# First MLP product of an encoder block: each weight tile's products written as three 256-column matmuls into half a bank, and the addition of two halves left out

## The reference

```
x  = x + merged @ w_out
h2 = rms_norm(x, g_mlp)
x  = x + jnp.square(jax.nn.relu(h2 @ w_mlp_in)) @ w_mlp_out
out = rms_norm(x, g_final)
```

## Time and profile before

| | |
|---|---|
| median of 3 runs | 1630.17 us (1629.72 to 1630.33) |
| the profiled execution | 1630.46 us |
| its span, first to last instruction | 1628.6 us |
| PE busy | 1616.6 us (99%), 7974 matmuls |
| PEld busy | 1361.0 us (84%) |
| DVE busy | 1215.4 us (75%) |
| ACT busy | 898.4 us (55%) |
| granted TensorE clock, mean | 0.999 of full speed |

### The profile page before, as it was taken

How to read it: one execution, slowest core, us unless ns; L and a number is a source line. 1 busy time by engine, 2 the same in 40 slices (tenths; PEclk the granted TensorE clock), 3 DMA queues, 4 the chain that set the end, 5 groups by cost and what they waited for, 6 DMA issues and landing times.

```text
span 1628.6 us, 20399 instructions
## 1 busy us (share of the span) xinstructions
PE 1616.6 (99%) x7974; PEld 1361.0 (84%) x7974; DVE 1215.4 (75%) x1470; ACT 898.4 (55%) x1248; POOL 79.0 (5%) x67
## 2 busy tenths in 40 slices
PE   9999999999999999999999999999999999999998
PEld 7888888888888888888888888888888888888886
DVE  7887778877666677766565567996699768986793
ACT  6666656766565445554444555654565455555562
POOL 3000000000000134000000000000000000000000
PEclk9999999999999999999999999999999999999999
DMA  7666665666556664445565775457635863576461
GB/s 270 193 207 201 187 188 188 206 195 205 174 186 185 190 186 154 143 143 179 182 234 193 259 235 190 157 206 235 190 125 202 273 190 130 207 262 189 144 233 52
DMA packets 134192, 312.19 MB, mean 192 GB/s; under 512 B 9744, under 2 KB 10448, under 8 KB 133968
## 3 DMA queue, kind: packets, MB, share of 16 engines
q1 hardware_dynamic: 129376, 302.21, 56.8%
q10 hardware_dynamic: 4720, 8.68, 2.1%
HBM read 308.68 MB, written 2.16 MB: 191 GB/s over the span
## 4 chain that ended last, share of the span: by engine, by line
PE 87%; DVE 9%; issue 2%; DMA 1%; ACT 1%; POOL 0%; POOLq 0%; ACTq 0%; DVEq 0%
PE G L1599 18%; PE G L1600 17%; PE G L1601 17%; PE S L1608 7%; PE G L1608 7%; PE G L1612 4%; PE S L1612 4%; PE S L1599 3%; PE S L1601 3%; PE S L1600 3%; DVE wlo L951 3%; DVE wlo_late L951 2%; PE S L1620 1%; DMA raw<-in_w_in 1%; DVE raw L954 1%
## 5 line engine op out<-in xcount | busy, mean ns | idle before, releaser
L602 ACT ACTIVATE whi<-raw 128x1024 fp32r<-128x1024 f32 x377 | 398.4, 1060 | 395.7 <-PE G L1601 317.0
L951 DVE TENSOR_TENSOR wlo<-raw,whi 128x1024 fp32r<-128x1024 f32 x377 | 461.0, 1236 | 133.6 <-ACT whi L602 132.8
L1599 PE MATMUL G<-whi,a_both 128*128 128x512 f32 x960 | 376.8, 393 | 2.2 <-DVE wlo L951 2.2
L1601 PE MATMUL G<-whi,a_both 128*128 128x512 f32 x960 | 373.8, 389 | 0.0
L1600 PE MATMUL G<-wlo,a_both 128*128 128x512 f32 x960 | 373.8, 389 | 0.0
L1599 PEld LDWEIGHTS G<-whi,a_both 128*128 128x128 f32 x960 | 180.3, 188 | 39.9 <-issue 2.8
L1601 PEld LDWEIGHTS G<-whi,a_both 128*128 128x128 f32 x960 | 180.2, 188 | 37.8
L1600 PEld LDWEIGHTS G<-wlo,a_both 128*128 128x128 f32 x960 | 180.4, 188 | 35.7
L1599 PE MATMUL G<-whi,b_hi 128*128 128x512 f32 x328 | 128.5, 392 | 0.3
L1600 PE MATMUL G<-wlo,b_hi 128*128 128x512 f32 x328 | 128.0, 390 | 0.0
L1601 PE MATMUL G<-whi,b_lo 128*128 128x512 f32 x328 | 127.7, 389 | 0.0
(11 more groups left out here) (283 smaller groups left out, 2591.7 us busy)
## 6 DMA issues: line engine op xcount, KB each, us to landing
raw<-in_w_in SPq DMA_DIRECT2D x208, 512.0 KB, 4.1
raw<-in_w_mlp_in SPq DMA_DIRECT2D x64, 512.0 KB, 4.3
gates<-in_w_mlp_in SPq DMA_DIRECT2D x64, 512.0 KB, 3.7
raw<-in_w_mlp_out SPq DMA_DIRECT2D x64, 512.0 KB, 4.9
gates<-in_w_mlp_out SPq DMA_DIRECT2D x64, 512.0 KB, 4.9
raw<-in_w_ssm_up SPq DMA_DIRECT2D x32, 512.0 KB, 3.6
raw<-in_w_attn_up SPq DMA_DIRECT2D x32, 512.0 KB, 4.0
raw<-in_w_out SPq DMA_DIRECT2D x32, 512.0 KB, 4.6
```

Of the source, the lines that this page charges most:

```text
L602: act.activation(high(m), piece(n), ACT.Copy).then_inc(hi_made, 1)
L951: dve.tensor_tensor(low(m), piece(n), high(m).bitcast(F32), ALU.subtract).then_inc(lo_made, 1)
L1599: pe.matmul(out_ap, hi[:, k, cols], w_hi, start=start, stop=False)
L1601: return pe.matmul(out_ap, lo[:, k, cols], w_hi, start=False, stop=stop)
```

## The change

`weights_first` now issues, for each tile c and contraction step kk, three matmuls of 256 moving columns into the first half of the bank: high weights by `a_hi`, high weights by `a_lo`, low weights by `a_hi`. The second half of each bank is no longer used. ACT's copy of it (L887), DVE's addition of the halves (L1382) and their semaphores `hid_t` and `h_taken` are gone. DVE's maximum and product (L1384) reads PSUM itself and waits for the window's matmuls itself, and PE's waits for free banks are on `hid_v`. The scratch tile `s_sum` shares `tmp_a` with the copy that is gone; the wait that guarded it moved from ACT to DVE, ahead of the sums of the blocks.

```diff
         def hidden(p, idx, pr, pp):
             g, j = idx
-            if p == 0:
-                act.wait_ge(used, done(pr, pp))
-                if g or j > CROSSED[0]:
-                    act.wait_ge(s_lo_made, len(CROSSED) * g + sum(u < j for u in CROSSED))
-                act.activation(hidden_t, hidden_banks(j)[:, :, T:2 * T], ACT.Copy).then_inc(hid_t, 1)
             if p == 1:
...
         def hidden(p, idx, pr, pp):
             g, j = idx
             if p == 0:
-                dve.wait_ge(hid_t, g * 4 + (j + 1))
+                dve.wait_ge(used, done(pr, pp))
                 if 4 * g + j:
                     dve.wait_ge(hid_lo, g * 4 + j)
                 dve.wait_ge(hid_hi, g * 4 + (j + 1))
-                dve.tensor_tensor(hidden_u, hidden_t, hidden_banks(j)[:, :, 0:T], ALU.add).then_inc(h_taken, 1)
-                dve.wait_ge(h_taken, g * 4 + (j + 1))
-                dve.scalar_tensor_tensor(out=hidden_u, in0=hidden_u, scalar=0.0,
+                dve.scalar_tensor_tensor(out=hidden_u, in0=hidden_banks(j)[:, :, 0:T], scalar=0.0,
                                          in1=rstd_row[:, :].unsqueeze(1).to_broadcast([P, 4, T]),
                                          op0=ALU.max, op1=ALU.mult).then_inc(hid_v, 1)
...
-                turn = 4 * (len(CROSSED) * g + CROSSED.index(j))
+                before = len(CROSSED) * g + CROSSED.index(j)
+                turn = 4 * before
+                if before:
+                    dve.wait_ge(s_lo_made, before)
...
             for c in range(4):
-                cols = [slice(kk * N + c * P, kk * N + (c + 1) * P) for kk in range(2)]
                 for kk in range(2):
-                    pe.matmul(banks[:, c, :], high(m)[:, cols[kk]],
-                              a_both[:, 2 * p + kk, :, :].rearrange("p h t -> p (h t)"),
-                              start=(p + kk == 0), stop=False)
-                for kk in range(2):
-                    last = pe.matmul(banks[:, c, 0:T], low(m)[:, cols[kk]], a_hi[:, 2 * p + kk, :],
-                                     start=False, stop=(2 * p + kk == KT - 1))
+                    cols, k = slice(kk * N + c * P, kk * N + (c + 1) * P), 2 * p + kk
+                    pe.matmul(banks[:, c, 0:T], high(m)[:, cols], a_hi[:, k, :], start=(k == 0), stop=False)
+                    pe.matmul(banks[:, c, 0:T], high(m)[:, cols], a_lo[:, k, :], start=False, stop=False)
+                    last = pe.matmul(banks[:, c, 0:T], low(m)[:, cols], a_hi[:, k, :], start=False, stop=(k == KT - 1))
             return last
...
             if kind == "mlp_in" and idx[1] > 1:
-                pe.wait_ge(h_taken, 4 * idx[0] + (idx[1] - 1))
+                pe.wait_ge(hid_v, 4 * idx[0] + (idx[1] - 1))
```

More of the change, by code:

```diff
@@ L440, in build @@
     merge_v, fin_v, fin_a = sem("merge_v"), sem("fin_v"), sem("fin_a")
-    hid_t, hid_v, hid_sq, hid_hi, hid_lo = [sem(n) for n in ("hid_t", "hid_v", "hid_sq", "hid_hi", "hid_lo")]
+    hid_v, hid_sq, hid_hi, hid_lo = [sem(n) for n in ("hid_v", "hid_sq", "hid_hi", "hid_lo")]
     row_mm = sem("row_mm")
     t_made, s_v, s_hi_made, s_lo_made = sem("t_made"), sem("s_v"), sem("s_hi_made"), sem("s_lo_made")
-    h_taken, c_taken = sem("h_taken"), sem("c_taken")
+    c_taken = sem("c_taken")
     mix_a, mix_v, x_mixed = sem("mix_a"), sem("mix_v"), sem("x_mixed")
@@ L491, in hidden_banks @@
         return S if j % 2 else G
-    hidden_t = tmp_a[:, :, :].rearrange("p b (c t) -> p (b c) t", c=2)
     s_sum = tmp_a[:, :, :].rearrange("p b (i t) -> p (b i) t", i=2).rearrange("p i (k t) -> p i k t", k=2)
@@ L1839, in pair_window @@
                     if q == 0:
-                        pe.wait_ge(h_taken, 4 * g + 3)
+                        pe.wait_ge(hid_v, 4 * g + 3)
                         pe.wait_ge(hid_lo, 4 * g + 3)
@@ L1845, in pair_window @@
                     if q == 0:
-                        pe.wait_ge(h_taken, 4 * g + 4)
+                        pe.wait_ge(hid_v, 4 * g + 4)
                         pe.wait_ge(s_lo_made, len(CROSSED) * (g + 1))
```

## The result

The changed kernel takes 1642.42 us (median of 4 runs, 1642.27 to 1642.62) for 1630.22 us before: +12.2 us, a ratio of 1.0075 with a 95% interval of 1.0063 to 1.0088. It is slower, and the forecast was 1640.5.

What follows compares the result with a forecast made beforehand. PE was taken to bound the kernel: 512 patterns at +20.4 ns give +10.4 us, all ACT, DVE and wait terms 0, so 1640.5 us on the median, range 1629 to 1649.

Steps and rivals of the forecast that it cites:

- PE bounds the windows, the rest is idle: `mlp_in` windows: PE busy in all of 22.29 us, so work taken off ACT and DVE is worth 0.
- The cost per matmul: First MLP product: 119.5 ns per 256-column matmul, 717.0 ns a pattern for 696.6, +10.4 us over 512 patterns.
- the inner steps' 120: Attention's run of six 256-column matmuls: the second to the sixth start 120 ns apart.
- the run's mean of 118.3: Attention's run of six: 0.71 us until the next matmul's start, 118.3 ns each, first step included.
- The first argument of the section: Changed pattern: six instructions, each some 13.3 ns beyond its columns, make 120 ns a matmul and 720 a pattern.
- The run's short first step: Attention's run of six: its first step is 110 ns, used with 115 ns for a lower bound of 113.
- settles lower: Rival: the long 256-column stream takes 116.7 ns a matmul, +1.8 us, 1632 us, about the same; chance 0.18.
- the small product's 116.7 ns: Early small product: twelve 256-column matmuls with 128- and 64-column loads by turns take 1.40 us, 116.7 ns each.
- The short step: Rival: an unmixed 256-column stream keeps 113 ns a matmul, -9.5 us, 1621 us, faster; chance 0.07.
- The bill that is put off: Rival: the stream itself pays what short runs leave to later matmuls, 124 ns each, +24 us, 1654; chance 0.13.
- The wait moved to DVE and the waits on `hid_v`: DVE's wait on `s_lo_made` and PE's waits for free banks in the MLP windows: worth 0.
- The 0.4 us at each of the three places: `mlp_pair`: PE's first matmul of the next half is late behind `add_sums`; at most 1.2 us won, taken as 0.

Runs made afterwards that it cites:

- `vectors_alone`: The changed kernel with the old wide and narrow matmuls, without ACT's copy and DVE's addition, against the kernel before: 1630.20 us for 1629.92, ratio 1.0001.
- `load_64`: The changed kernel with loads of 64 columns instead of 128 in the first MLP product, 256 moving columns kept: 1623.25 us.
- `wide_first`: The kernel before with all eight 512-column matmuls of a piece first, then all eight of 256 columns: 1630.90 us for 1629.92, ratio 1.0006.

## Why the prediction was right

- *PE bounds the windows, the rest is idle*: right. PE is busy in 92.15 of 92.15 us, and `vectors_alone` shows the vector engines' part to move the time by 0.3 us, with zero well inside the interval.
- *The cost per matmul*: right for what the change does, each matmul with its own full load keeping 13.3 ns beyond its columns; its size was 0.5 ns short. I took 119.5 ns between the inner steps' 120 and the run's mean of 118.3; the long stream has 120.0 from its third step on (its first starts, in the timeline, are at 932.28, 932.39, 932.51 and 932.63 us). 6 x 0.5 x 512 = 1.5 us is the distance from the forecast's +10.4 to the measured +11.9. The first argument of the section, 13.3 ns beyond the columns for each instruction, had given 720 ns a pattern and would have been exact. The run's short first step was not a part of the rate. That 13.3 ns is a fixed cost of an instruction, as one may read there, the runs don't bear out: with 256 columns it was 6.7 with half loads, and with 192 columns the floor took its place.
- *The rivals*: "settles lower" rested on the small product's 116.7 ns, and what spoke against it decided: half of its loads are short, and `load_64` has 113.3 for these. "The short step" (113 ns) appears only as the very first step of the stream, at 932.28 us, and not again. "The bill that is put off" was misread by me. In the earlier trace rows seven wide matmuls behind a narrow run take 724.17 - 722.55 = 1.62 us for 7 x 226.5 = 1586 ns, so they are some 34 ns late. Such a lateness is paid once for each return to wide ones, as `wide_first` shows with 27 ns behind eight narrow ones. It doesn't belong to each narrow matmul, and 124 ns was no real bound.
- *The wait moved to DVE and the waits on `hid_v`*: worth 0, as said; the second product's stretch changed by 0.07 us. The 0.4 us at each of the three places stayed: in the timeline PE's starts there are 0.52 us apart before and 0.53 to 0.54 after, where they are otherwise 0.23.
- *The rule of the Trainium skill*, "TensorE: Matmul & The Clock Gate", section "Back-to-back issue gap": its N / 2.4 + 2.5, given for an isolated warm gap, makes an estimated 109.2 ns for 256 columns, and the measured stream of loads and matmuls has 120.0. The trace decides; here the part beyond the columns is 13.3 ns for 256 and 384 columns with full loads, and 13.2 for 512. The prediction's "5 to 13 ns or more" beside this rule doesn't follow from its 118 to 120 and 226.5 ns, which leave 11 to 13.
- *The load*: the prediction left open whether load or columns set the step. With full loads, 192 and 224 columns take the same 111.7 ns, and with half loads 192 columns take 88.6 ns, so there the full load decides. At 256 columns the step is above the floor, and yet half a load makes it 113.3 ns for 120.0: the load isn't wholly hidden there either. The Trainium skill, "TensorE: Matmul & The Clock Gate", section "LDWEIGHTS (loading the stationary operand)", has 128 / 1.2, an estimated 107 ns for a full load, which comes near the measured floor and 5 ns below it.

## What to carry to other kernels

In the streams measured here (fp32r, full loads, granted clock 1.00, 192 to 512 moving columns of one width) a step is the longer of 111.7 ns and the columns plus 13.3 ns. So a 512-column matmul cut into two costs 13.3 ns in such a stream. Here it was 11.7 ns each (23.3 for two), as the uniform stream has lost the 3.3 ns that the mixed pattern paid. The cost comes even when the cut saves work on other engines, and that work is worth only what it holds up on the path that sets the end. Where the rate of a new pattern is to be taken from a short run in the trace, take its inner steps: its first step and what it leaves to the matmuls behind it belong to the change of pattern, not to the rate.

## What the runs showed of the hardware that was not expected

- Four matmuls of mixed widths cost up to 13 ns more than the sum of their own rates, by their order alone (706.6 ns by turns, 696.6 two and two, for 693.3).
- A shorter load is not always a cheaper one: with 256 moving columns, 128, 64 and 32 loaded columns make steps of 120.0, 113.3 and 117.8 ns, all 192 steps of a window lying close to these means.
- PEld's busy share says little about the limit. It is 100% of the window with 384 moving columns (22.19 of 22.19 us) and with 192 alike, but only the second is held up by the load. By the groups of PEld a full load's record is 188 ns long with 384 columns and 192 ns with 192, so it reads as always busy wherever the steps are shorter than that.
